# Pool projection first in a layer, and the second half of the stick-breaking heads inside the attention loop

## The reference, cut to what matters

```python
def hybrid_layer(x, ...):
    hn = rms_norm(x, norm1_g)
    proj = jnp.einsum('bsd,df->bsf', hn, w_in)
    ya = mla_mixer(...)                # 8 heads, softmax attention
    yb = stick_breaking_mixer(...)     # 4 heads of 64
    yc = pool_mixer(proj[..., o4:], pool_w, pool_scale)
    x = x + jnp.einsum('bsm,md->bsd', concatenate([ya, yb, yc]), w_out)
    return x + hier_moe(rms_norm(x, norm2_g), ...)   # 32 experts, 2 per token

def stick_breaking_mixer(q, k, v):     # per block of 128 queries
    z = einsum('bqhd,bkhd->bhqk', q, k) * scale
    strict = pos[k] < pos[q]
    log_1m_beta = where(strict, -softplus(z), 0)
    between = cumsum(log_1m_beta, reverse=True) - log_1m_beta
    a = where(strict, exp(log_sigmoid(z) + between), 0)
    out = einsum('bhqk,bkhd->bqhd', a, v)
```

## Time and profile before

| | us |
|---|---|
| median of 3 runs | 1381.53 (1381.42 to 1381.89) |
| the profiled execution | 1376.42 |
| its span in the trace | 1374.5 |
| PE busy | 1218.1 (89%) |
| DVE busy | 441.1 (32%) |
| ACT busy | 391.6 (28%) |
| POOL busy | 29.8 (2%) |

### The profile page before, as it was taken

One profiled execution on the slowest core, in us unless ns is written; L12 is line 12 of the kernel. 1 busy time (PEld: TensorE's weight loads), 2 busy tenths in 40 slices (PEclk: granted clock), 3 DMA queues, 4 the chain that ended last, 5 costly groups with the idle time before them and its releaser, 6 DMA issues.

```text
span 1374.5 us, 18357 instructions
## 1 busy us (share of the span) xinstructions
PE 1218.1 (89%) x7770; PEld 928.0 (68%) x7770; DVE 441.1 (32%) x882; ACT 391.6 (28%) x751; POOL 29.8 (2%) x44
## 2 busy tenths in 40 slices
PE   5999999999999799999989979877789897987776
PEld 3999998877578799999775745433258584452233
DVE  4444544240630544455355121000023713110002
ACT  4333343132541443333145221000113513110002
POOL 0000000100010000000020000000001100000000
PEclk9999999999879899999997989997899998999887
DMA  9455453622102355544230789999976525999993
GB/s 379 169 180 183 159 180 123 228 102 93 62 1 92 142 187 189 187 165 174 92 153 1 311 354 422 423 423 422 423 306 271 218 93 220 422 424 422 422 424 144
DMA packets 44903, 322.43 MB, mean 235 GB/s; under 512 B 5144, under 2 KB 5400, under 8 KB 6672
## 3 DMA queue, kind: packets, MB, share of 16 engines
q1 hardware_dynamic: 43440, 314.45, 57.8%
q0 software_dynamic: 688, 3.69, 0.8%
q10 hardware_dynamic: 688, 3.05, 0.6%
HBM read 320.09 MB, written 3.16 MB: 235 GB/s over the span
## 4 chain that ended last, share of the span: by engine, by line
PE 69%; DMA 20%; DVE 7%; ACT 2%; issue 1%; SPq 1%; ACTq 0%; DVEq 0%
PE bank L1070 10%; PE bank L1027 9%; PE bank L1028 9%; PE bank L1029 9%; DMA ring<-in_stream 8%; PE bank L1037 6%; DMA arena<-in_stream 6%; DMA xn<-in_stream 4%; PE bank L1475 3%; PE bank L1454 3%; PE bank L1104 3%; DMA sm<-in_stream 2%; PE bank L1080 2%; PE bank L1494 2%; PE bank L990 2%
## 5 line engine op out<-in xcount | busy, mean ns | idle before, releaser
L1027 PE MATMUL bank<-r_hi,w_hi 128*128 128x272 f32 (+1 forms) x1056 | 303.0, 287 | 17.1 <-DVE r_lo L1595 13.9
L1028 PE MATMUL bank<-r_lo,w_hi 128*128 128x272 f32 (+1 forms) x1056 | 303.9, 288 | 0.0
L1029 PE MATMUL bank<-r_hi,w_lo 128*128 128x272 f32 (+1 forms) x1056 | 302.9, 287 | 0.0
L1027 PEld LDWEIGHTS bank<-r_hi,w_hi 128*128 128x128 f32 x1056 | 201.7, 191 | 18.4 <-issue 18.3
L1589 DVE TENSOR_TENSOR w_lo<-ring,w_hi 128x2048 fp32r<-128x2048 f32 x66 | 151.3, 2292 | 177.1 <-ACT w_hi L691 177.1
L1029 PEld LDWEIGHTS bank<-r_hi,w_lo 128*128 128x128 f32 x1056 | 201.6, 191 | 0.0
L1028 PEld LDWEIGHTS bank<-r_lo,w_hi 128*128 128x128 f32 x1056 | 200.8, 190 | 0.0
L691 ACT ACTIVATE w_hi<-ring 128x2048 fp32r<-128x2048 f32 x66 | 126.1, 1912 | 143.1 <-PE bank L1029 138.6
L1070 PE MATMUL bank<-xn,ring 128*128 128x256 f32 (+1 forms) x624 | 143.0, 387 | 8.1 <-DVE xn L1580 8.1
L1070 PEld LDWEIGHTS bank<-xn,ring 128*128 128x128 f32 x624 | 118.4, 192 | 30.8 <-issue 12.0
L1926 DVE TENSOR_TENSOR arena<-arena,bank 128x256 f32<-128x256 f32 x16 | 6.7, 421 | 247.8 <-ACT arena L930 247.8
(11 more groups left out here) (299 smaller groups left out, 1216.7 us busy)
## 6 DMA issues: line engine op xcount, KB each, us to landing
ring<-in_stream SPq DMA_DIRECT2D x160, 1024.0 KB, 4.9
arena<-in_stream SPq DMA_DIRECT2D x68, 1024.0 KB, 26.1
sm<-in_stream SPq DMA_DIRECT2D x18, 1024.0 KB, 26.8
G<-in_stream SPq DMA_DIRECT2D x10, 1024.0 KB, 24.8
w_ukv<-in_stream SPq DMA_DIRECT2D x10, 1024.0 KB, 26.0
sq<-in_stream SPq DMA_DIRECT2D x10, 1024.0 KB, 26.6
xn<-in_stream SPq DMA_DIRECT2D x10, 1024.0 KB, 26.3
mixT<-in_stream SPq DMA_DIRECT2D x8, 1024.0 KB, 26.6
```

Source lines behind the costliest of these rows:

```text
L1027: mm(dst, hi, r_hi[:, k, 0:T], start=first, stop=False)
L1028: mm(dst, hi, r_lo[:, k, 0:T], start=False, stop=False)
L1029: return mm(dst, lo, r_hi[:, k, 0:T], start=False, stop=last)
```

## The change

In each layer of the second kind:

- The columns of w_in are put in another order, so that the pool channels are the first two units; latents are units 2 to 4, the rope key 5, stick-breaking queries and keys 6 to 9, values 10. POOL's chain waits for unit 1 instead of unit 10.
- Of the stick-breaking heads the first half of the chain stays ahead of the loop: z, -|z|, exp, Ln. The second half, softplus, suffix sums, subtraction, exp, output product, save, moves into the attention loop, one head every two steps, as a stage `stick` on PE, DVE and ACT. Its results go to `stick_bank(h)`: bank 1 for heads 0 and 2, bank 3 for heads 1 and 3.
- ACT does exp and Ln of all heads behind its query copies, with no copies between them.
- The pool product moves from step 8 to step 12, and the first half of the output projection waits for all four heads.
- `ln` and `zm` move to the arena slots `S_AR + 4` and `S_AR + 5`, which now open when all heads are saved. The other two arena slots open at the first transpose, which no longer waits for the heads to be saved but for z to be read.

The diff, cut (the three `stick` stages are those of ACT, PE and DVE, in this order):

```diff
-        POOL_AT = [SEG_M[l][0] + 8 for l in range(LAYERS)]
+        def stick_bank(h):
+            return bank[1 + 2 * (h % 2)]
+
+        POOL_AT = [SEG_M[l][0] + 12 for l in range(LAYERS)]
...
+            if j in (S_AR + 4, S_AR + 5):
+                return [("stick_saved", SH * (l + 1)), ("pool_d_ready", 2 * l + 1)]
             return [("aT_ready", m0 + 1), ("pool_d_ready", 2 * l + 1)]
...
-                unit_free(pool, l, 10)
+                unit_free(pool, l, 1)
...
+                def stick(g):
+                    h, at_ = divmod(g - SEG_M[l][0] - 2, 2)
+                    if 0 <= h < SH and at_ == 0:
+                        act.wait_ge(S("stick_log_ready"), SH * l + h + 1)
+                        copy(ln[:, h, :], zm[:, h, :], ACT.Exp).then_inc(S("stick_ready"), 1)
+                    h -= 1
+                    if 0 <= h < SH and at_ == 0:
+                        b = 64 * (h % 2)
+                        act.wait_ge(S("stick_o_ready"), SH * l + h + 1)
+                        copy(mixT[b:b + 64, 4 + h // 2, 0:T2], stick_bank(h)[b:b + 64, 0:T2], ACT.Copy
+                             ).then_inc(S("stick_saved"), 1)
...
-                steps(SEG_M[l], (save_T, 2), (save_o, 3), (exps, 0), (save_pool, 0))
+                steps(SEG_M[l], (save_T, 2), (save_o, 3), (exps, 0), (stick, 0), (save_pool, 0))
...
                 def turn_m(g):
                     if g < SEG_M[l][0] + 2:
-                        pe.wait_ge(S("stick_saved"), SH * (l + 1))
+                        pe.wait_ge(S("nabs_ready"), SH * (l + 1))
                     turn(g)
+
+                def stick(g):
+                    h, at_ = divmod(g - SEG_M[l][0] - 1, 2)
+                    if 0 <= h < SH and at_ == 0:
+                        if h >= 2:
+                            pe.wait_ge(S("stick_saved"), SH * l + h - 1)
+                        pe.wait_ge(S("softplus_ready"), SH * l + h + 1)
+                        dst = stick_bank(h)
+                        mm(dst[:, T2:384], upper, ln[:, h, T2:384], start=True, stop=True)
+                        mm(dst[:, 0:T2], upper, ln[:, h, 0:T2], start=True, stop=True)
+                        mm(dst[:, P:T2], ones, ln[:, h, T2:384], start=False, stop=True,
+                           skip_group_check=True).then_inc(S("later_ready"), 1)
+                    h -= 1
+                    if 0 <= h < SH and at_ == 0:
+                        b = 64 * (h % 2)
+                        dst = stick_bank(h)
+                        pe.wait_ge(S("stick_ready"), SH * l + h + 1)
+                        mm(dst[b:b + 64, 0:T2], vb[:, 0, 64 * h:64 * h + 64], ln[:, h, 0:T2], start=True, stop=True)
+                        mm(dst[b:b + 64, P:T2], vb[:, 1, 64 * h:64 * h + 64], ln[:, h, T2:384], start=False, stop=True,
+                           skip_group_check=True).then_inc(S("stick_o_ready"), 1)
...
-                steps(SEG_M[l], (scores, 0), (pool_mix, 0), (first_half, 1), (turn_m, 2), (pv, 3))
+                steps(SEG_M[l], (scores, 0), (stick, 0), (pool_mix, 0), (first_half, 1), (turn_m, 2), (pv, 3))
...
+                def stick(g):
+                    h, at_ = divmod(g - SEG_M[l][0], 2)
+                    if 0 <= h < SH and at_ == 0:
+                        dve.wait_ge(S("ln_ready"), SH * l + h + 1)
+                        V.scalar_tensor_tensor(ln[:, h, :], zm[:, h, :], 0.0, ln[:, h, :], ALU.max, ALU.add
+                                               ).then_inc(S("softplus_ready"), 1)
+                    if 0 <= h < SH and at_ == 1:
+                        dve.wait_ge(S("later_ready"), SH * l + h + 1)
+                        V.tensor_tensor(zm[:, h, :], zm[:, h, :], stick_bank(h)[:, 0:384], ALU.subtract
+                                        ).then_inc(S("stick_log_ready"), 1)
+
+                steps(SEG_M[l], (weights, 2), (maxes, 0), (stick, 0))
```

More of the change, by code:

```diff
@@ L848, in v @@
                     return bank[u % 4][:, 0:T2]
[L850 to L862, removed]
                 act.wait_ge(S("pad_ready"), l + 1)
                 for t in range(2):
-                    save(u0 + 9 + t, lambda: copy(upad[:, t, 16:272], v(9 + t), ACT.Copy))
-                for h in range(SH):
-                    nc.scalar.activation(ln[:, h, :], ln[:, h, :], ACT.Ln, bias=1.0).then_inc(S("ln_ready"), 1)
+                    save(u0 + t, lambda: copy(upad[:, t, 16:272], v(t), ACT.Copy))
+                for t in range(2):
+                    save(u0 + 2 + t, lambda: copy(cq[:, t, :], v(2 + t), ACT.Copy),
+                         lambda: copy(sq[:, t, 0:T2], v(2 + t), ACT.Square))
+                save(u0 + 4, lambda: copy(ckv[:, 0, :], v(4), ACT.Copy), lambda: copy(sq[:, 2, 0:T2], v(4), ACT.Square))
+                save(u0 + 6, lambda: copy(qbT[:, 0, :], v(6), ACT.Copy))
+                take_root(bank[7][0:64, 0:T2], G_EPSL, "head_sums", 3 + l)
+                save(u0 + 7, lambda: copy(qbT[:, 1, :], v(7), ACT.Copy))
+                for t in range(2):
+                    save(u0 + 8 + t, lambda: copy(kbT[:, t, :], v(8 + t), ACT.Copy))
+                save(u0 + 10, lambda: copy(vb.rearrange("p t n -> p (t n)"), bank[2][:, :], ACT.Copy))
                 for n in range(4):
@@ L1345, in _ @@
                     query_unit(16 + 2 * r, 768 + P * r)
-                for h in range(SH):
-                    pe.wait_ge(S("softplus_ready"), SH * l + h + 1)
-                    mm(bank[4 + h][:, T2:384], upper, ln[:, h, T2:384], start=True, stop=True)
-                    mm(bank[4 + h][:, 0:T2], upper, ln[:, h, 0:T2], start=True, stop=True)
-                    mm(bank[4 + h][:, P:T2], ones, ln[:, h, T2:384], start=False, stop=True,
-                       skip_group_check=True).then_inc(S("later_ready"), 1)
                 for n in range(4):
@@ L1778, in _ @@
                                            ).then_inc(S("nabs_ready"), 1)
-                for h in range(SH):
-                    dve.wait_ge(S("ln_ready"), SH * l + h + 1)
-                    V.scalar_tensor_tensor(ln[:, h, :], zm[:, h, :], 0.0, ln[:, h, :], ALU.max, ALU.add
-                                           ).then_inc(S("softplus_ready"), 1)
                 for r in range(2):
@@ L1791, in _ @@
                                         ALU.add).then_inc(S("q_rope_saved"), 1)
-                for h in range(SH):
-                    dve.wait_ge(S("later_ready"), SH * l + h + 1)
-                    V.tensor_tensor(zm[:, h, :], zm[:, h, :], bank[4 + h][:, 0:384], ALU.subtract
-                                    ).then_inc(S("stick_log_ready"), 1)
                 for n in range(4):
@@ L1800, in _ @@
                     V.tensor_copy(kcat[0:64, 2 * n + 1, :], src[64:128, 0:T2]).then_inc(S("unit_read"), 1)
-                steps(SEG_M[l], (weights, 2), (maxes, 0))
+                def stick(g):
[9 more added lines that the diff above has]
+                steps(SEG_M[l], (weights, 2), (maxes, 0), (stick, 0))
                 residual(3 + l if l == 0 else 4, 3, 1.0)
```

66 lines of the change are left out of this document (28 added, 38 removed).

## The result

The changed kernel takes 1398.67 us (median of 4 runs, 1395.61 to 1400.86), the kernel before 1381.71 us on the same chip (1381.42 to 1381.99). The ratio is 1.0114, with a 95% interval of 1.0089 to 1.0139: slower by 1.1%. Of the forecast, slower came true, and the time lies at the upper edge of its own range (1384 to 1399). The forecast was +9.8 us, measured were +17.0 by the medians and +19.2 by the profiled executions (1395.61 against 1376.42; spans 1393.7 and 1374.5).

What follows compares the result with a forecast made beforehand. Expert stages were taken as DMA-bound, so mixer changes pass straight through: layer 0 +11.0 less 8.0, layer 1 +12.0 less 5.2, together +9.8 us, making 1386.2 profiled or 1391.3 on the median. Range 1377 to 1401, the forecast's own 1384 to 1399.

Steps and rivals of the forecast that it cites:

- What bounds the kernel: Whole kernel: expert stages are DMA-bound, so every microsecond a mixer ends earlier or later moves the end by one.
- The slot waits: SP's queue: two arena slots open at step 10 instead of 0, costing nothing, since the next issue awaits the output projection.
- Up to Q nothing moves: Mixer up to PE's first query unit (Q): same work ahead, price 0, or 0.4 us if an ACT copy came late.
- From Q to the loop: First query unit to attention loop: start at Q + 14.7 us, 8.0 us earlier in layer 0, 5.2 in layer 1.
- The hand-off (b): Loop, banks 1 and 3: set h waits for ACT's save of head h - 2; two steps take 4.7 us at full clock.
- The sum of the loop, at a given clock: scores(0) to scores(10): 19.8 us at full clock, 29.4 at half; before, 14.82 and 13.81.
- the price of a step: PE's own work in loop steps 0 to 9: 0.92 us for each step of 128 keys at full clock.
- The tail: scores(10) to the output projection: 10.3 us against 9.06, pool product adding 0.9 and its ACT save 0.3.
- Which clock: PE in the loop: neither full nor half clock could be excluded, so half the difference, 24.6 us to scores(10).
- Rival 1: Loop: the clock stays up; -2.6 us in layer 0, +1.2 in layer 1, total -1.4, 1380 us; chance 0.15.
- Rival 2: Loop: the clock is at half all through; +8.9 and +12.6 us, total +21.5, 1403 us; chance 0.10.
- Rival 3: Loop: bank hand-off hidden, clock up, PE's work alone binds, 26.4 us; total -8.8, 1372.7 us; chance 0.13.

Runs made afterwards that it cites:

- e7: The changed kernel plus small identity matmuls that nobody reads, in PE's holes ahead of and in the attention loop; 1382.8 us, 1.0005 of the kernel before.
- e5: The changed kernel with the old projection order, pool units last and POOL's chain again running behind Q; 1400.2 us, 1.0112 of the kernel before.
- e1: The changed kernel with ACT's save of each stick-breaking head one step earlier, ahead of the next head's exp; 1388.2 us, 1.0031 of the kernel before.
- e9: The changed kernel with two suffix-sum sets ahead of the loop, new steps, output products paired and a dummy exp; 1366.1 us, 0.9897 of the kernel before.
- e6: The kernel before plus small identity matmuls that nobody reads, ahead of the value units and in loop steps 1 to 7; 1377.7 us, 0.9967 of it.
- e8: The changed kernel with sets in steps 1, 3, 7, 9, output products in pairs and the log subtraction later; 1380.3 us, 0.9984 of the kernel before.

## Why the prediction was right or wrong, point by point

- **What bounds the kernel.** Right. The expert stages kept their length, and 16.7 of the 19.2 us that the profiled execution lost lie between Q and the output projection. The slot waits were covered as said: SP's issue into the ring came 8.7 us later, with the output projection (767.82 against 759.17), and the experts, 0.4 us aside, as far behind it as before.
- **Up to Q nothing moves.** Right, by 0.1 us.
- **From Q to the loop.** Right: Q + 13.9 to 15.7 was foretold, 14.91 and 15.69 measured, 14.13 at full clock (e7). The waits are those named: 1.90 us for the key copies of bank 3 (2.2 foretold), 0.88 for the vm copy, which ends at 721.96 (0.7 foretold; the profile puts this wait down to "issue"). The rope additions took 1.76 a group, and with the POOL chain back beside them 3.68 (e5).
- **The hand-off (b).** The mechanism was right, down to the engine and the place: ACT's save, which stands last in its step, is waited for twice in each layer, by 0.97 and 1.28 us. Doing the save a step earlier takes both waits away (e1).
- **The sum of the loop, at a given clock.** Too small. At full clock it was to be 19.8 us to scores(10), and e7 took 21.45. By the prediction's own parts: up to the third set 9.8 us (9.4 foretold), from there to the fourth 5.15 (4.7), from the fourth to scores(10) 6.5 (5.7). The terms that were mis-sized: the first set takes 0.98 us and the other three 1.07 to 1.08 (priced 0.88, from sets that stood in a row), and an output product by itself 0.80 at full clock and 1.47 at half (priced 0.66 and 1.31, from the ratio of the columns). That makes 0.7 + 0.6 = 1.2 of the missing 1.65 us. Most of the rest is the price of a step: all ten were taken at 0.92, but steps 8 and 9 have 256 keys, and in layer 1 of the kernel before step 9 already took 1.10. The rule on packing from the Trainium skill, "TensorE: Matmul & The Clock Gate", Part 3, that I weighed here, agrees with the runs: the pairs taken apart cost even more than double, 1.60 us against 0.75 for two heads, and 0.81 when e9 put them together again.
- **The tail.** Priced at 10.3 us, measured 9.62 in both layers: the pool product cost 0.6 and its save nothing.
- **Which clock.** The level was too high in the forecast, and this and the sum above are the two steps that came out too small. I took half of the difference between the levels. The clock was at 0.50 for 21.4 us of the stage up to scores(10) in layer 0 and for 17.1 in layer 1. All of the stage at half was priced at 29.4, so these are 0.73 and 0.58 of it, which between the forecast's ends of 19.8 and 29.4 makes 26.8 and 25.4. Measured were 28.79 and 27.40. In the mixers, 6.9 us were missed: 2.2 + 0.8 by the clock in the loop, 2.0 + 2.0 by the terms above, 1.2 by a later start of the loop (15.69 in layer 1, the half-clock end), less 1.4 in the tail. So the terms of the loop missed 4.0 us and the clock 4.2, and a part was hidden by the tail, which was priced too high. I had argued that denser matmuls among the small ones could keep the clock up; the first set began at half clock in layer 0 (0.79 us for what is 0.49 at full), which the clock had had since 719.69, ahead of the loop, and sets that stand alone between holes of 0.6 to 1.3 us did not bring it back.
- **The rivals.** Rival 1 (clock up, 1380) is what e7 forces, by fillers: at full clock the two mixers take 90.4 us, 1.1 more than in the profiled execution of before where it said 1.4 less, and e7's whole time is that of the kernel before. Without fillers the clock didn't stay up in the profiled execution of the changed kernel. Rival 2 (half all through, 1403) lay nearer to the result than the forecast's centre did, by 4 us against 7. Rival 3 (hand-off hidden) is refuted for this kernel: both waits are in the trace, and at full clock the loop took 31.07 us and not 26.4. Nor does taking the wait away give what it said: at full clock e1's loop is 19.55 us up to scores(10), where rival 3 had 15.3 + 1.2 = 16.5. The hand-off was 1.9 to 2.3 us of the distance, not all of it.
- **What I did not see.** The question "what is the work worth where it goes" I answered with instruction times only. At full clock the four sets and four output products of before took 5.0 us ahead of the loop (4 x 0.88 + 1.50); in the loop they took 11.0 (21.45 less 10.4, the loops of e7 and e6 up to scores(10), e6's 11.21 less its own fillers, and the pool product had even left this part). Between Q and the loop only 5.8 us came free (19.93 less 14.13), and the tail grew by 0.6: 5.8 us a layer lost. e1 gives 1.9 to 2.3 of these to the hand-off, e8 takes away 3.7 with the late log and the pairs as well; how the last 2.1 divide is open. e9 shows the part of it that was to be had: the same products in holes that PE has anyway, and the pairs left whole.

## What to carry to other kernels

Work that is moved into a loop to fill it should go where the engine idles and keep what makes it cheap in one piece (pairs of 64 columns, sets in a row); taken apart, here it cost 5.8 us a layer at equal clock. When a chain crosses engines inside a loop, put the link that frees a bank ahead of the links that nobody waits for: one moved save took away two waits of 1.0 and 1.3 us in each layer. Compare stages at equal granted clock before blaming a structure, and get that number by filling the holes with matmuls whose result is dropped; but see that each stands in a real hole, since nine in e6's loop brought 0.8 us of their own.

## What the hardware showed that I had not expected

- Dropped matmuls make a kernel faster. 19 of them in each layer, in the holes of PE, gave the kernel before 0.33% (interval 0.12% to 0.55%); 25 took the changed one from 1.0114 to 1.0005 of it.
- TensorE's granted clock fell to half behind short holes. In layer 0 of the changed kernel it fell at 719.69; the longest hole of PE since Q was the 1.90 us that ended at 718.54. In layer 1 of before it fell at 1086.1, 8.8 us behind the end of a hole of 3.12 us and behind a stretch in which PE was idle for 0.78 us in all. In e6 and e7, with fillers in the holes, it stayed at 1.00; which of the holes brings it down, no run here separates.
- The same kernel scatters by more than its first runs told. The 4 runs of before lay within 0.6 us; in later sessions 31 runs of it went from 1372.7 to 1388.7. The mean granted clock goes with the time: it was 0.935 in the shortest of the 31 and 0.924 in the longest. Not every difference between stages is the clock: from the experts of layer 0 to the next mixer the changed kernel took 18.27 us at a mean clock of 0.82, e9 18.37 at 1.00, and e6 22.22 at 0.77. So differences under 0.3% in these runs are read from stages, not from the whole time.
